# Attention pairs on TensorE: a pair's value products moved behind the next pair's turns, turned probabilities in four buffers

## The reference

```
def windowed_gqa_sink(...):       # "window": 256 queries, 512 keys (256 latent in a band, 256 context), a sink per head
    p = softmax(concatenate([s_win, s_ctx, sinks]))
    o = einsum(p[..., :kw], vb) + einsum(p[..., kw:kw + C], vc)

def _mixer_ab(...):               # "ab": 8 heads of block attention, 8 of dilated attention, causal, 256 keys
    oa = _moba(...); ob = _dilated(...)

def _mixer_nsa(...):              # "nsa": per head three softmaxes over the same queries
    o = gates[0] * o_cmp + gates[1] * o_slc + gates[2] * o_win
```

## Time and profile before

| | us |
|---|---|
| median of 3 runs | 2571.49 |
| lowest, highest | 2565.56, 2571.93 |
| profiled execution, its time | 2567.2 |
| its span, first to last instruction | 2565.0 |
| TensorE (PE) busy | 2477.7 (97%) |
| VectorE (DVE) busy | 1334.0 (52%) |
| ScalarE (ACT) busy | 1155.3 (45%) |
| window attention, stretch of the span | 1527.3 to 1586.4 |
| ab attention | 1864.0 to 1923.9 |
| nsa attention | 2254.9 to 2324.7 |

### The profile page before, as it was taken

The page is one execution under the profiler, slowest core; times in us unless marked ns, Lnnn a source line. Parts: engine busy times, 40 slices in busy tenths (PEclk is TensorE's granted clock), DMA queues, the critical chain, the costliest instruction groups (busy, mean ns, idle before and its releaser), DMA issues.

```text
span 2565.0 us, 40626 instructions
## 1 busy us (share of the span) xinstructions
PE 2477.7 (97%) x16133; PEld 2123.5 (83%) x16133; DVE 1334.0 (52%) x2003; ACT 1155.3 (45%) x1827; POOL 23.7 (1%) x37
## 2 busy tenths in 40 slices
PE   7999999999999999999999999999979999979998
PEld 5777788886777778777788876999859999868998
DVE  4322334896523233432333367655776666876665
ACT  4333323465433332333322347664566655665654
POOL 0000000000000000000000000000100001000000
PEclk9999999999999999999999999999999999989999
DMA  8444552210344433244422231455425554413554
GB/s 325 164 164 173 189 178 90 91 50 1 115 174 180 169 147 109 104 164 175 181 103 101 95 115 36 178 196 197 168 83 179 188 206 178 175 50 113 197 194 153
DMA packets 52727, 374.93 MB, mean 146 GB/s; under 512 B 5822, under 2 KB 7034, under 8 KB 8736
## 3 DMA queue, kind: packets, MB, share of 16 engines
q1 hardware_dynamic: 50000, 358.63, 38.3%
q0 software_dynamic: 2208, 14.37, 1.6%
q10 hardware_dynamic: 432, 0.73, 0.1%
HBM read 372.55 MB, written 7.39 MB: 148 GB/s over the span
## 4 chain that ended last, share of the span: by engine, by line
PE 88%; DVE 6%; ACT 2%; DMA 1%; issue 1%; POOL 0%; ACTq 0%; DVEq 0%; POOLq 0%; SPq 0%
PE acc L1899 27%; PE acc L1900 26%; PE acc L1901 26%; PE bank L1982 2%; DVE wlo L1346 1%; DMA raw<-in_slabs 1%; DVE prod L630 1%; PE bank L2009 1%; PE acc L2414 1%; DVE split_x L1431 1%; PE acc L2388 1%; DVE sc L1800 1%; DVE prod L1717 1%; ACT sc L1236 0%; ACT pT L1256 0%
## 5 line engine op out<-in xcount | busy, mean ns | idle before, releaser
L1346 DVE TENSOR_TENSOR wlo<-raw,whi 128x1024 fp32r<-128x1024 f32 x534 | 645.7, 1223 | 870.6 <-ACT whi L806 870.1
L806 ACT ACTIVATE whi<-raw 128x1024 fp32r<-128x1024 f32 x534 | 556.2, 1056 | 930.9 <-PE acc L1901 872.5
L1899 PE MATMUL acc<-split_x,whi 128*128 128x256 f32 (+1 forms) x2808 | 935.5, 333 | 13.8 <-DVE split_x L1431 9.5
L1900 PE MATMUL acc<-split_x,whi 128*128 128x256 f32 (+1 forms) x2808 | 920.6, 328 | 0.0
L1901 PE MATMUL acc<-split_x,wlo 128*128 128x256 f32 (+1 forms) x2808 | 920.6, 328 | 0.0
L1899 PEld LDWEIGHTS acc<-split_x,whi 128*128 128x128 f32 x2808 | 528.1, 188 | 100.8 <-issue 36.3
L1901 PEld LDWEIGHTS acc<-split_x,wlo 128*128 128x128 f32 x2808 | 527.8, 188 | 50.0
L1900 PEld LDWEIGHTS acc<-split_x,whi 128*128 128x128 f32 x2808 | 528.1, 188 | 48.8 <-issue 1.7
L1899 PE MATMUL acc<-split_g,whi 128*128 128x512 f32 (+1 forms) x1056 | 351.3, 333 | 0.0
L1901 PE MATMUL acc<-split_g,wlo 128*128 128x512 f32 (+1 forms) x1056 | 351.1, 333 | 0.0
L1900 PE MATMUL acc<-split_g,whi 128*128 128x512 f32 (+1 forms) x1056 | 351.1, 332 | 0.0
(11 more groups left out here) (290 smaller groups left out, 2246.3 us busy)
## 6 DMA issues: line engine op xcount, KB each, us to landing
raw<-in_slabs SPq DMA_DIRECT2D x329, 1024.0 KB, 4.8
ada_raw<-in_slabs SPq DMA_DIRECT2D x10, 1024.0 KB, 25.6
skew_dram<-lines_dram POOLq DMA_DIRECT2D x1, 6144.0 KB, 24.8
bt<-skew_dram POOLq DMA_DIRECT2D x4, 1024.0 KB, 9.6
x<-in_x_in SPq DMA_DIRECT2D x1, 2048.0 KB, 17.7
mlp<-in_slabs POOLq DMA_DIRECT2D x2, 1024.0 KB, 6.2
out<-x SPq DMA_DIRECT2D x1, 1024.0 KB, 4.8
rope<-in_rope POOLq DMA_DIRECT2D x1, 512.0 KB, 3.8
```

The lines of the kernel that those rows point to most:

```text
L806: nc.scalar.activation(whi[:, n % 2, cols], raw_of(n, cols), ACT.Copy).then_inc(ready, 1)
L1346: nc.vector.tensor_tensor(wlo[:, n % 2, cols], raw_of(n, cols), whi[:, n % 2, cols].bitcast(F32), ALU.subtract).then_inc(low, 1)
L1899: nc.tensor.matmul(out, w[0], xx[0], start=first, stop=False)
L1900: nc.tensor.matmul(out, w[0], xx[1], start=False, stop=False)
```

## The change

`turned_in` is new and gives each unit one of four buffers, by u modulo 4: the two of `pT` for 0 and 1, and for 2 and 3 space that holds nothing more at that time: tiles 8 to 11 of `QK` in nsa (keys, copied to `kd` before), `kraw` in window (keys, copied to `kd` too), `Pc` in ab (used by nsa only). C(k) no longer waits for V(k-1) but for V(k-2). TensorE's iteration becomes S(k+3), T(k), (in nsa the turns of `Pc`), V(k-1).

```diff
+        def turned_in(st, u):
+            if u % 4 < 2:
+                return pT[:, u % 2, :]
+            if st.what == "nsa":
+                return QK[:, 8 + 2 * (u % 2):10 + 2 * (u % 2), :].rearrange("p a t -> p (a t)")
+            return kraw[:, u % 2, :] if st.what == "window" else Pc[:, u % 2, :, :].rearrange("p a b -> p (a b)")
...
                     act.wait_ge(t_ready, 6 + A0 + u + 1)
-                    act.wait_ge(pv_done, A0 + u + 1)
-                    nc.scalar.activation(pT[:, u % 2, 0:keys], turn_bank(st, u)[:, 0:keys], ACT.Copy)\
+                    if u >= 4:
+                        act.wait_ge(pv_done, 2 + A0 + u - 3)
+                    nc.scalar.activation(turned_in(st, u)[:, 0:keys], turn_bank(st, u)[:, 0:keys], ACT.Copy)\
                         .then_inc(pt_ready, 1)
...
-                            ins = nc.tensor.matmul(out(v), vt[:, at:at + HD], pT[:, v % 2, P * j:P * j + P],
+                            ins = nc.tensor.matmul(out(v), vt[:, at:at + HD], turned_in(st, v)[:, P * j:P * j + P],
...
                 for u in range(0, UNITS, 2):
                     if u + 6 < UNITS:
                         scores(u + 6)
-                    if u:
-                        values(u - 2)
                     for v in (u, u + 1):
                         turned(v)
                         if ab and v < 24:
...
                             value_step(1 + v // 8, 2 * (v % 8) + 1)
                     if nsa and u in (0, 2):
                         pc_turned(u // 2)
+                    if u:
+                        values(u - 2)
                 values(UNITS - 2)
```

## The result

The changed kernel took 2555.64 us (median of 10 runs, 2552.73 to 2566.62), the kernel before, on the same chip, 2571.71 us (10 runs, 2564.62 to 2574.13): a ratio of 0.9946, 95% interval 0.9934 to 0.9958. The profiled executions differ by 13.5 us (2553.68 against 2567.2; spans 2551.5 and 2565.0). The forecast was 2560.0 in a range of 2551 to 2567.

A forecast was written before the change was run, and what follows sets the result against it. A ring of ScalarE and VectorE without TensorE was taken to bound window's and nsa's middles; 3.0 (window) + 0 (ab) + 3.5 + 2.2 (nsa) = 8.7 us gave 2558.2 or 2562.5, so 2560.0, range 2551 to 2567.

The forecast's parts named there:

- Window, start: Window attention up to H(0): T(1) no longer stands behind V(0); 0.8 us gained, bounds 0 to 2.1.
- Window, middle: Window attention's steady laps: waits for C are slack, 0 us gained, at most the rest of the 6.0.
- the circle of ScalarE and VectorE: H, L, N, B, E, C, H sets the lap without TensorE: 6.36 us in window, 6.84 in nsa.
- Window, tail: End of the window attention: the chain from C(13) ends at 1584.2 instead of 1586.4, 2.2 us gained.
- ab: The ab attention: one bank for turns, end waits for L(6); 0 us, bounds 1 lost to 1.5 gained.
- nsa, start: Start of nsa: T(1) runs inside the wait for the compressed copy, V(1) behind T(2); 3.5 us, bounds 3.0 to 5.1.
- nsa, middle: Steady laps of nsa: the ring of waits keeps its 6.84 us, 0 us gained.
- first rival: All attentions: the whole wait of V for C is cost, 21.5 us vanish, 2545.7 us; chance 0.07.
- nsa, tail: End of nsa: 4.5 us gained at full clock, 0.7 at half clock; 2.2 taken.
- second rival: Only window's tail 2.2 and nsa's start 3.0 come, 5 us: 2562 or 2566.3; chance 0.19 with the fourth.
- The fourth: T is late for N, not C, so waits only change name; 2564.2 if throughout; chance counted with the second.
- third rival: TensorE's waits gather ahead of T and the clock drops, 24 us lost against 8.7 gained: 2582.5; chance 0.06.

The follow-up runs named there:

- e5: Against the kernel before: four buffers everywhere, the new TensorE order in the window attention alone; ratio 0.9978 to the kernel before.
- e8: The changed kernel plus filler matmuls of constants in nsa that keep TensorE at work during two idle times; ratio 0.9947 to the kernel before.
- e9: The changed kernel run again, unaltered; 2562.27 us, ratio 0.9960 to the kernel before.
- e10: The changed kernel with ScalarE copying nsa's turned compressed probabilities ahead of the exponentials E(3) and E(4); ratio 0.9944 to the kernel before.
- e2: Against the changed kernel: new order in window and nsa with the two old buffers, ab left as before the change; ratio 0.9993 to the kernel before.
- e4: The kernel before with L moved behind N and B in VectorE's order, old TensorE order and two buffers; ratio 1.0001 to the kernel before.
- e11: The changed kernel with e10's early copy and L moved behind N and B on VectorE; 2547.85 us, ratio 0.9910 to the kernel before.

## Why the prediction was right, point by point

- **Window, start (0.8 taken, 0 to 2.1).** Measured 0.85, and 0.83 to 0.85 in e5, e8 and e9. In e10 the clock of window's start fell and took as much away again (18.49).
- **Window, middle (0 taken, most: the rest of the 6.0).** Measured 0.87 us, always the same. This term was mis-sized, and the step behind it was wrong: that the circle of ScalarE and VectorE contains no instruction of TensorE. B waits for T as well, for its buffer in `probs`, and T stood behind a V that waited for C. The waits of VectorE in window's middle, the kernel before (two rows), then the changed one:

```profile
DVE Vm L1800 <- PE acc L2388: 1.0, 2, 0.6
...
DVE sc L1800 <- PE acc L2388: 0.4, 1, 0.4
```

```profile
DVE olo L1844 <- ACT ohi L1270: 2.4, 4, 0.7
```

Before, B waited three times for T, 1.4 us together. In the changed kernel it never does, and VectorE waits for H alone, once in four of the five laps: only now is the circle closed without TensorE. With four buffers and the old order (e1) the three waits and the 33.56 us are there unchanged; with the order and two buffers (e2) the middle is 32.70. Before, the five laps took 6.36, 7.89, 6.76, 6.28 and 6.27, now they take 6.22, 7.63, 6.41, 6.21 and 6.22. 0.61 of the 0.87 us comes from the second and third; in the second ScalarE, which has two splits of weights there, is now busy for all of the 7.63 us, and before for 7.75 of 7.89. In nsa's middle VectorE waited for T neither before nor after, so there the step held.
- **Window, tail (2.2).** Measured 2.24. The chain worked out from C(13) (V(15) done and wo begun 5.7 us on) came true: C(13) at 1576.50, wo at 1582.20, 5.7 us on.
- **ab (0, bounds -1 to 1.5).** Middle and tail unchanged to 0.01 us. The 1.4 us by which it grew are ahead of H(0), where the clock was low: 0.66 in the first 5 us after, 1.00 before. Rows by stretch for these, the kernel before, then the changed one:

```profile
1864.00:1869.00 5.00, 4.91 (x42) 4.61 (x43) 1.82 (x12) 3.39 (x10) 0.00 (x0) 1.00 0.90 352
```

```profile
1859.00:1864.00 5.00, 4.91 (x29) 4.31 (x30) 1.83 (x12) 3.40 (x10) 0.00 (x0) 0.66 0.92 378
```

- **nsa, start (3.5, bounds 3.0 to 5.1).** Measured 3.7 in the profile pair. Over all, old order 25.08, 25.03, 23.74, 25.24, new order 21.36, 20.26, 22.58: means of 24.8 and 21.4, a gain of 3.4. At about the same clock of the start it is 2.5 (25.08 at 0.86, 22.58 at 0.85) or 2.4 and 3.5 (23.74 at 0.93, 21.36 and 20.26 at 0.92), so the 3.0 that the prediction took for certain was a little too much in two of these three pairs.
- **nsa, middle (0).** Measured 0.01, though 8.0 us of waits for C still end in it (9.1 before). It decides against the first rival, 2545.7 us: the waits were slack, and renaming them bought nothing. The spacing of H, which the prediction named as the judge, is 6.83.
- **nsa, tail (2.2 from 4.5 at full clock and 0.7 at half).** Measured 3.0. At full clock the prediction had wo 5.9 us behind C(13), which is 4.95 behind H(5); e9 and e10 show 4.94 and 4.93. What I mis-sized was how much of it the clock takes: it recovered sooner. The order's own part is 1.4 to 1.7 us (e8 above); that the rest came on top is the clock of this execution, and luck. V(13) and most of T(15) still ran at the lower level (1.93 us for T(15), 1.17 in e9), V(14) and V(15) at the upper:

```profile
2305.55 0.89 PE L2397 MATMUL acc<-const,QK 128*128 128x128 f32 x4 [2.41 <-ACT QK L1265]
...
2308.39 1.93 PE L2397 MATMUL acc<-const,sc 128*128 128x128 f32 x8
...
2312.25 0.38 PE L1908 MATMUL acc<-ohi,whi 128*128 128x256 f32 x1
```

- **The sum.** 8.7 us were taken; the attentions gave 9.3 in the profile pair, or 10.7 without ab's 1.4. Over all profiles they gave 3.9 (window) + 6.6 (nsa: 69.1 on the mean of four with the old order, 62.6 of three with the new) + 0.1 (ab) = 10.6. The second rival, only the certain 5 us, falls by this as far as the profiles go, and by the first comparison's 16.1 us; e9's 7.0 us from the median alone would not have refuted it. The fourth falls too, as T in window and nsa is late for C mostly and only once or twice for N.
- **The third rival, slower by the clock.** It did not come: in the middles of window and nsa the changed kernel's clock stayed full, though waits of up to 1.3 us now stand ahead of T there. The Trainium skill, "TensorE: Matmul & The Clock Gate", section "A second HAM failure mode: psum-queue depth-cycling", tells of a clock that swings where TensorE idles shortly and often. The new order showed no swing in nsa's middle in any of eight profiles; the old order showed one lap at a lower clock in two of five (0.76 in e5, 0.80 in e4). Where it fell in nsa, the longest wait close before was between 1.2 us (e11's start) and 4.2, but such waits did not bring it down each time: at the same wait of 2.41 us e9 kept it in the tail where the changed kernel's first profile lost it, and at the same wait of 2.13 us in the first lap the kernel before kept it and e5 did not. The prediction names 1.35 us as the idle time that the middle bore; it bore 2.13 too. So such a wait is at most a risk.
- **From the profile to the median.** The point 2560.0 was set about halfway between 2558.2 and 2562.5. The first comparison gave 16.1 us, the second 7.0, with the same two kernels. The attentions give about 10.6 on the mean of the profiles. What is left is 5.5 in the first comparison and -3.6 in the second, so it does not belong to the change. The slower dense work of the last section, 8 us in some executions, is large enough for it; that it accounts for the medians is not shown. The measured median lies 4.4 us under the point, and part of that is such luck.

## What to carry to other kernels

A wait that ends with X says nothing of its worth until you know what X is waiting for: look for the lap time of the circle, and if it has no instruction of the waiting engine in it, expect the middle of the loop to keep its pace and count the gain only at its start and end, where the circle isn't closed. Check that against the waits of the circle's own engines: in nsa VectorE never waited for T and the middle gained nothing; in window it did, for 1.4 us, and the middle gained 0.87. Put the consumer that can wait behind the producer that others wait for, and give it the buffers in the same edit; then look again at the circle, since slack created by the new order (here for L) may open it. Where laps are equal and no engine is full in them (79% in nsa's middle here), look for an order to change, not for work to cut.

## What the runs showed of the hardware

In 11 of 13 profiled executions the dense matmuls of 128x256 between ab and nsa follow each other at the same pace; in e2 and e9 they are 4% slower, at a granted clock of 1.00, and TensorE never idle. The rows of the changed kernel, then of e9 (the same program; the stretch, its length, busy us and matmuls of TensorE, granted clock, DMA share, GB/s), the last one a stretch ahead of ab:

```profile
1950.00:1970.00 20.00, 20.00 (x179) 1.00 0.60 210
2010.00:2030.00 20.00, 20.00 (x179) 1.00 0.50 174
```

```profile
1950.00:1970.00 20.00, 20.00 (x171) 1.00 0.56 199
2010.00:2030.00 20.00, 20.00 (x172) 1.00 0.50 164
...
1700.00:1720.00 20.00, 20.00 (x179) 1.00 0.56 179
```

That is 20 us / 179 = 0.112 us a matmul against 20 / 172 = 0.116. It was there in all of the stretches looked at from 1950 to 2110, and is gone in the dense work behind it; it makes the gap 337.0 us in e9 and 338.8 in e2 instead of 328.5 to 332.5. 8 us is more than half of what the change gains, and it hides or doubles a gain of that size in single runs. What starts it no run here shows. Beside it the granted clock is at its lower level for short stretches, at the start of ab and ahead of and in nsa's start in most profiles, but at places and lengths that differ for the same program: that moved the start of ab between 20.2 and 23.1 us.
